# A decoder layer on one core: softmax pipeline, sample steps, output projection and weight split arranged differently

## What is computed

```
def swa_attend(q, k, v, q_pos, k_pos, sinks):        # 16 heads of 64, 4 heads share a key/value head
    s = einsum('bnqkgd,bnskd->bnkgqs', q, k) * 64 ** -0.5
    s = s - slopes * (q_pos - k_pos)                  # ALiBi; masked outside a window of 128
    m = maximum(max(s), sink)
    p = exp(s - m)
    denom = sum(p) + exp(sink - m)
    return einsum('bnkgqs,bnskd->bnqkgd', p / denom, v)

o = swa_attend(...)      # prompt: 4 blocks of 128 queries against 256 keys
                         # sample: 8 queries of each sequence against 128 cached and 8 new keys
y = x + o @ w_out
```

## Time and profile before

| what | us |
|---|---|
| median of 3 runs (1464.42 to 2238.26) | 1465.75 |
| span of the profiled execution | 1458.1 |
| TensorE matmul busy in it | 1385.9 (95%) |
| VectorE busy | 521.3 (36%) |
| ScalarE busy | 394.0 (27%) |
| GpSimd busy | 572.6 (39%) |

### The profile page before, as it was taken

The page is one execution under the profiler, slowest core; times in us unless marked ns, Lnnn a source line. Parts: engine busy times, 40 slices in busy tenths (PEclk is TensorE's granted clock), DMA queues, the critical chain, the costliest instruction groups (busy, mean ns, idle before and its releaser), DMA issues.

```text
span 1458.1 us, 23961 instructions
## 1 busy us (share of the span) xinstructions
PE 1385.9 (95%) x9812; PEld 1292.0 (89%) x9812; DVE 521.3 (36%) x886; ACT 394.0 (27%) x668; POOL 572.6 (39%) x249
## 2 busy tenths in 40 slices
PE   6888789999999999999999999979999999999995
PEld 6766538999999999999789789769999999999995
DVE  6466654621111111222125666647311111111114
ACT  3233331222222222222102534422222222222221
POOL 3422203633333333444556343327333333334441
PEclk9999858999999999999999999999999999999998
DMA  6500000222222222222322132212222222222221
GB/s 226 203 30 30 30 0 32 85 82 77 86 86 79 79 86 86 89 86 88 116 73 83 62 109 105 102 48 87 87 79 79 86 72 86 86 87 87 87 72 65
DMA packets 34341, 121.00 MB, mean 83 GB/s; under 512 B 4993, under 2 KB 6337, under 8 KB 32849
## 3 DMA queue, kind: packets, MB, share of 16 engines
q1 hardware_dynamic: 30496, 103.43, 21.7%
q10 hardware_dynamic: 3792, 16.82, 3.1%
HBM read 112.77 MB, written 9.44 MB: 84 GB/s over the span
## 4 chain that ended last, share of the span: by engine, by line
PE 70%; issue 13%; POOL 8%; DVE 7%; ACT 2%; DMA 0%; POOLq 0%; ACTq 0%; DVEq 0%
PE ps L372 22%; PE ps L374 22%; PE ps L373 22%; POOL wlo L341 4%; POOL whi L338 4%; DVE SC L844 2%; DVE SC L823 1%; ACT SC L1190 1%; PE ps L510 1%; DVE SC L820 1%; PE ps L508 1%; DVE rbc L771 1%; PE ps L501 1%; PE ps L482 0%; DVE nm L827 0%
## 5 line engine op out<-in xcount | busy, mean ns | idle before, releaser
L341 POOL TENSOR_TENSOR wlo<-wst,whi 128x1024 fp32r<-128x1024 f32 x188 | 465.1, 2474 | 505.7 <-ACT whi L1254 501.3
L372 PE MATMUL ps<-xhi,whi 128*128 128x288 f32 x1840 | 551.5, 300 | 1.9 <-DVE QT L789 0.9
L373 PE MATMUL ps<-xlo,whi 128*128 128x288 f32 x1840 | 544.7, 296 | 0.0
L374 PE MATMUL ps<-xhi,wlo 128*128 128x288 f32 x1840 | 542.8, 295 | 0.0
L372 PEld LDWEIGHTS ps<-xhi,whi 128*128 128x128 f32 x1840 | 346.7, 188 | 10.7 <-issue 9.4
L374 PEld LDWEIGHTS ps<-xhi,wlo 128*128 128x128 f32 x1840 | 348.0, 189 | 0.0
L373 PEld LDWEIGHTS ps<-xlo,whi 128*128 128x128 f32 x1840 | 347.4, 189 | 0.2
L372 PE MATMUL ps<-hhi,whi 128*128 128x288 f32 x960 | 286.0, 298 | 7.1 <-POOL wlo L341 3.3
L373 PE MATMUL ps<-hlo,whi 128*128 128x288 f32 x960 | 284.3, 296 | 0.0
L374 PE MATMUL ps<-hhi,wlo 128*128 128x288 f32 x960 | 283.4, 295 | 0.0
L338 POOL TENSOR_TENSOR whi<-wst,epsz 128x1024 fp32r<-128x1024 f32 x56 | 107.2, 1914 | 353.6 <-PE ps L374 347.4
(11 more groups left out here) (165 smaller groups left out, 1076.6 us busy)
## 6 DMA issues: line engine op xcount, KB each, us to landing
wst<-w_blocks_in SPq DMA_DIRECT2D x189, 512.0 KB, 3.3
S<-s_in ACTq DMA_DIRECT2D x4, 1024.0 KB, 4.9
s_sample_out<-S ACTq DMA_DIRECT2D x4, 1024.0 KB, 3.9
y_out<-x SPq DMA_DIRECT2D x8, 288.0 KB, 2.3
bias<-bias_in ACTq DMA_DIRECT2D x1, 2048.0 KB, 10.9
x<-x_in SPq DMA_DIRECT2D x6, 288.0 KB, 7.2
ktx<-ktx_in ACTq DMA_DIRECT2D x1, 1024.0 KB, 6.2
Vc<-vc_in ACTq DMA_DIRECT2D x1, 1024.0 KB, 13.2
```

Of the source, the lines that this page charges most:

```text
L341: nc.gpsimd.tensor_tensor(wlo[:, slot % RING, :], wst[:, slot, :], raw(whi[:, slot % RING, :]), ALU.subtract).then_inc(w_split, 1)
L372: mm(out, stat[0], mov[0], start=start, stop=False)
L373: mm(out, stat[0], mov[1], start=False, stop=False)
L374: return mm(out, stat[1], mov[0], start=False, stop=stop)
```

## The change

- A step's heads are scored one at a time into one bank (4 or 5); the second waits on the first (`first_head`). Other matmuls (`fill`) stand between. Scores of step k+1 are issued in round k, together with transposes and values of step k-1.
- Three score buffers; VectorE does `biased(k)`, then `probs(k-1)`. Scores, bias and sinks are negated (ScalarE turns the tables once), so the minimum is the exponent's bias and L827 goes. Outputs of prompt tiles alternate between banks 2 and 7.
- Sample steps hold four sequences and one key/value head each; their values come out transposed already, so the copy `OS` and `turn_out` go. Four of them stand in tile 4 between its prompt steps, four at the end.
- The first half of the output projection (4 of 8 input chunks) is cut in 16 units of 12 matmuls, issued from tile 7 on and added to x by VectorE each; the second half follows as 8 tiles of 24 matmuls.
- Weight blocks 4 to 15 are split by ScalarE (high) and VectorE (low) (`early`); GpSimd does the others as before. Small tables are loaded by SP ahead of block 4.

```
+def attention_steps():
...
+    out = [("p", n, i) for n in range(4) for i in range(NQB)]
+    for i in range(NQB):
+        out += [("p", 4, i), ("s", i)]
+    return out + [("p", n, i) for n in range(5, 8) for i in range(NQB)] + [("s", q) for q in range(4, 8)]
...
+def attention_fills():
...
+            room = [(k - 1, n > 0, 2), (k, 0, 1), (k, 1, 1), (k + 1, 0, 1), (k + 1, 1, 2), (k + 2, 0, 1)]
...
+    k = AT_STEP["p", 7, 0]
+    room = [(k - 1, 1, 1)] + [(k + i, part, 1) for i in range(4) for part in range(2)]
+    room += [(k + 4 + i, part, 2) for i in range(4) for part in range(2)]
+    room += [(NSTEP, 0, 1), (NSTEP, 1, 1), (NSTEP + 1, 0, 2), (NSTEP + 2, 0, 3)]
...
+SPLIT_AT = {6 + n: AT_STEP["p", n, 0] for n in range(6)}
+SPLIT_AT.update({12: AT_STEP["p", 6, 0], 13: AT_STEP["p", 7, 0], 14: NSTEP - 4, 15: NSTEP - 1})
...
+            def scores(k, hd):
+                bank = 4 + k % 2
...
+                    if hd == 1:
+                        pe.wait_ge(first_head, 4 * n + i + 1)
+                    ins = mm(ps[:, bank, 256 * hd + c0:256 * hd + 256], QT[q, n, i * P:(i + 1) * P],
+                             KT[q, n // GRP, k0:(i + 1) * P], start=True, stop=True)
...
+            for k in range(-1, NSTEP + 3):
+                if k + 1 < NSTEP:
+                    scores(k + 1, 0)
+                fill(k, 0)
+                if 1 <= k <= NSTEP:
+                    turn(k - 1)
+                if k + 1 < NSTEP:
+                    scores(k + 1, 1)
+                fill(k, 1)
+                if 1 <= k <= NSTEP:
+                    values(k - 1)
...
+            def early(n):
...
+                dve.wait_ge(early_hi, n + 1 - EARLY)
+                tt(wlo[:, n % RING, :], wst[:, n % STAGE, :], raw(whi[:, n % RING, :]),
+                   ALU.subtract).then_inc(early_split, 1)
...
-                    chain.link(ins)
-                    ts(nm[:, par, :], mx[:, par, :], -1.0, None, ALU.mult).then_inc(sm_done, 1)
...
+            for k in range(END):
...
+                        tt(xu, ps[:, u % 3, 0:H], xu, ALU.add).then_inc(unit_read, 1)
...
+                if k < NSTEP:
+                    biased(k)
...
+                        read_tile(("Q", n), B_Q + n, 0, cols(QT, n), -HD ** -0.5)
...
+                if 1 <= k <= NSTEP:
+                    probs(k - 1)
...
+                    if SPLIT_AT[n] + 1 == k:
+                        early(n)
```

More of the change, by code:

```diff
@@ L356, in _ @@
                 laps = (n1 - m0) // STAGE
-                with pool.Fori(0, laps) as r:
-                    for j in range(STAGE):
-                        n = m0 + j
-                        split(r * STAGE + n, n % STAGE, r + (n // STAGE + 1), False, own, r * STAGE + (k0 + n - n0))
+                if laps:
+                    with pool.Fori(0, laps) as r:
+                        for j in range(STAGE):
+                            n = m0 + j
+                            split(r * STAGE + n, n % STAGE, r + (n // STAGE + 1), False, own, r * STAGE + (k0 + n - n0))
                 for n in range(m0 + laps * STAGE, n1):
@@ L472, in scores @@
[L472 to L483 removed]
+                    q = slice(HD * hd, HD * hd + HD)
@@ new lines, in turn @@
+            def turn(k):
+                SC = SCs[k % 3]
+                pe.wait_ge(pr_done, k + 1)
+                if k >= 1:
+                    pe.wait_ge(pt_read, k)
+                if STEPS[k][0] == "p":
+                    for hd in range(2):
+                        for kc in range(0 if STEPS[k][2] else 1, 2):
+                            ins = mm(ps[:, 6, (2 * hd + kc) * P:(2 * hd + kc + 1) * P],
+                                     SC[:, hd, kc * P:(kc + 1) * P], ident[:, :], start=True, stop=True,
@@ L543, in _ @@
-            pe.wait_ge(o_lo, 16)
-            for m in range(KC):
+                    t, e = divmod(STEPS[k][1], 2)
+                    gg, bh = divmod(t, 2)
+                    h = slice((2 * gg + e) * HD, (2 * gg + e + 1) * HD)
+                    rows = slice(HD * e, HD * e + HD)
+                    if e == 0 and t >= 1:
+                        pe.wait_ge(*((o_lo, 8) if t == 3 else (os_lo, t)))
+                    mm(ps[rows, SAMPLE_BANK[t], 0:P], V[0:NS_TOK, NQB, h], PTs[0:NS_TOK, par, 1, :],
+                       start=True, stop=False)
@@ L1176, in _ @@
             act.dma_start(io["v_kept"], io["v_cache"][:, NT:WIN, :]).then_inc(s_out, 16)
+            for n in range(B_Q, B_Q + 2):
+                early(n)
+            act.wait_ge(s_attc, 16 * N_ATTC)
+            act.wait_ge(s_rows, 16 * N_ROWS)
+            fn(bias[:, :, :], bias[:, :, :], ACT.Copy, scale=-1.0)
+            fn(sbias[:, :, :], sbias[:, :, :], ACT.Copy, scale=-1.0).then_inc(bias_turned, 1)
             act.wait_ge(tile_read.sem, tile_read["K", 1])
```

477 lines of the change are left out of this document (268 added, 209 removed).

## The result

The changed kernel takes 1471.84 us (median of 20 executions, 1463.15 to 1479.37); the kernel before, on the same chip, 1463.15 (20 executions, 1458.76 to 1465.98 and one of 2238.26). The ratio is 1.0061, 95% interval 1.0043 to 1.0078: 0.6% slower, clear of the noise though small, where 1% faster was forecast. It lies 22 us above the forecast and 5 above the range. The executions of the changed kernel differ with the mean granted clock: those of 1463 us have 0.978, those of 1471 have 0.971 to 0.973, those of 1477 to 1479 have 0.966 to 0.969. The profiled one is among the shortest: 1464.09 us, span 1462.3, against a span of 1458.1 before.

The account below looks back on a forecast made before the run. TensorE was taken to lose 3.7 us a tile to VectorE, waiting for ScalarE and GpSimd. Gains of 35.2 us, less 9.3 and 7.2, less 3.5 for the clock, gave 15.2: 1450 us, range 1436 to 1467.

Parts of the forecast that it names:

- Part 3: Weight blocks 4 to 15 split on ScalarE and VectorE: hidden under TensorE's work, except a 2.0 us wait for block 15.
- Part 5: Second projection half and first FFN tile: VectorE bounds, accumulation ending behind GpSimd's work, 3.2 to 5.5 us per addition, 32.4 us.
- the allowance for the clock: Attention stretch: with less idling, 7 of some 20 us at the lower clock level remain, counted as 3.5 us.
- Part 1: Prompt steps: with the deeper pipeline VectorE no longer waits for exponentials; 1.65 us of TensorE idling per tile stays.
- Part 2: Prompt steps' scores: one head alone costs what two cost together, 0.63 us, adding 2.3 us per tile, 18.5 for eight.
- Rival (a): Prompt steps' scores: a head alone costs half, so Part 2 is 6.4 us, not 18.5; 1438 us, chance 0.20.
- no scaling over 1 us: Sign of being right in the new profile: none of VectorE's scalings in the attention takes over 1 us.
- Part 4: Sample steps: four in tile 4 add 9.3 us there; tile 7 to first FFN tile takes 78.9 instead of 114.1.
- Rival (b): Clock stays low from sample step 4 on, 29.5 us more: 1480 us, slower by 1%, chance 0.08.
- Rival (c): Splits and reads fall on VectorE's chain in each tile, uncovered: ten blocks, 23 us, 1473 us, chance 0.09.
- The sum: Whole kernel: gain of 15.2 us on a span of 1458.1 gives 1443, plus 7.6 from span to median: 1450 us.

Follow-up runs that it names:

- the version with all three edits: Changed kernel with heads scored side by side, blocks 16 to 19 split by ScalarE and VectorE, and query tile 5 spread over tile 4's steps: 1438.57 us, ratio 0.9846.

## Why the prediction was wrong

Three terms were too small: a wait that was put at nothing (Part 3), the bound of the second half (Part 5), and the time at the lower clock. No one of them makes up the 22 us. Held against the forecast, stage by stage in the execution of 1464.09 us (before the allowance for the clock); a stage begins with the first work of its first round on TensorE, for tile 7 the scores of its second block (191.67), for sample steps 4 to 7 the first matmul of round 36 (210.13):

| stage | forecast | measured | off |
|---|---|---|---|
| start of tile 7 | at 189.5 | at 191.67 | +2.2 |
| tile 7 | 16.4 | 18.5 | +2.1 |
| sample steps 4 to 7 | 22.0 | 27.2 | +5.2 |
| rest of the first half, last addition | 8.1 | 11.6 | +3.5 |
| second half and first FFN tile | 32.4 | 39.5 | +7.1 |

**Part 1 was right.** VectorE no longer waits for the exponentials, and idle time is left once a tile: 1.54 us (1.03 and 0.51), for 1.65. Tiles without a fall take 17.4 to 17.7 us, for 18.15. What wasn't seen is what this idle time does: it is what the clock falls on. And VectorE's waits for ScalarE, which the deeper pipeline was for, were the smaller part of the loss in the kernel before: with the split alone its tiles were 14.4 to 15.2 us apart.

**Part 2 was right**, and it was the largest cost that an edit brought back: 0.63 us for one head, as the earlier trace rows had it; undone, 1.9 to 2.1 a tile and 13 us or more in sum. Rival (a) is refuted by the same rows.

**Part 3 failed in its mechanism.** "GpSimd idles in the attention, so the earlier trace rows don't recur" holds up to 228 us and not beyond. The ring releases block 16 to GpSimd when block 14 has been used, and that is within the last sample step; a scaling took 1.87 us, where "no scaling over 1 us" was the sign of being right. The step had 2.0 us for block 15, and with GpSimd held back it is 2.09; the wait was 5.72. The other 3.6 us, and the lower clock behind them (13.7 us for 3.4), are the +5.2 and the larger part of the +3.5 of the table: 7.3 of these 8.7 us are gone in the profile with GpSimd held back. Of the execution's time 4.2 came back, since block 16 was then split beside the second half. Splits of blocks 4 to 14 on ScalarE and VectorE cost nothing that was found, and in the kernel before those of 4 to 11 bring 10 us.

**Part 4 was right in its work and wrong in its clock.** Tile 4 with four sample steps took 32.8 us for 27.4, since 17.1 us of it were at the lower clock. That is 5.4 too many, and the tiles around it gave 3 of them back, so 2.2 stand in the first row of the table. Tile 7 has the wait for `hlo` (1.15 us), which the forecast had not, and a fall of 3.4 us behind it (201.5). Sample steps 4 to 6 took 5.0 to 5.12 us for 5.1.

**Part 5 was right in its mechanism and too small.** VectorE behind GpSimd is the bound. But the forecast let only the accumulation be held up, and `xlo` is as well: 6.38 and 6.48 us for an output tile where 5.5 was the upper end. With the projection's blocks on ScalarE and VectorE only 0.6 us of the 7.1 came back (2.6 against the run that holds block 16 back), since GpSimd then split the FFN's first two blocks beside the same output tiles. So which share of the 7.1 is GpSimd's is not measured; that `xlo` and `acc` beside it take 1.2 and 2.2 us longer is.

**The clock.** 7 us at the lower level were allowed for, 41 are there in a short execution and 75 in a long one (65 in the profile of the kernel before). Part of it is in the stages above already. Rival (b) named the right engine state and the wrong place: in the short execution sample steps 4 to 6 were at full clock. The long executions reach 1477 to 1479, near its 1480, through falls in tiles 1 to 4 and in tile 7; that is not the way it forecast, so that the number is near is luck. Rival (c) was wrong: with TensorE's work in each step the chain isn't late.

**The sum** was made against one execution and put 7.6 us on top, the distance of a median of three. An execution lies some 1.8 us above its own span (1464.09 and 1462.3), and by twenty executions the median of the kernel before is 1463.15 and not 1465.75, 5.0 above the span. The changed kernel has a spread of its own, 8 us from the profiled execution to the median. For the span, 1443 was forecast and 1462.3 measured: 16.6 in the stages up to 288.44 (20.1 off, less the 3.5 allowed for the clock), and 2.7 behind them. There the profile has three falls of 3.4 us (710.1, 805.7 and 972.9), where that of the kernel before has one of 6.8 (706.7); that explains less than 2 of the 2.7.

**Not tried apart:** the deeper pipeline, the new layout of the sample steps and the split of the projection were never run alone, so what each of them brings or costs is known only through the rows.

## What to carry to other kernels

Before a helper engine is counted as idle, look up what releases its next piece of work, and what stands in the other engine's queue at that moment; here a split that nobody needed for 20 us held up one that TensorE was waiting for. When work is moved out of a stage, ask what it covered there: half of the projection's matmuls were the cover of VectorE's additions. And of five changes made together, run each alone: two thirds of one of them were worth 10 us alone, the one with the heads cost more than that, and with the two losses undone and the fills spread the version is 1.5% faster than the kernel before, 1438.57 us, and 1.9% with the useless matmuls, 1433.81.

## What the runs showed of the hardware

A TensorE that is idle once in 16 to 18 us for 1.5 to 2.0 us (1.03 and 0.51 above, 1.67 to 2.01 in the version with all three edits), and busy for 94% of the time, can have its granted clock fall behind each such idle time (0.97 or 0.85 in the same 58 us of the same kernel). It isn't the same in each execution: 1463 and 1479 us for the same program. Ten matmuls of 1.30 us on data of no use, in that place, made the best version 4.8 us faster by its median (6 executions each, with ranges that overlap), and the changed kernel 5.0 (1471.84 to 1466.87), of which only the longer executions are the reason (shortest 1463.15 and 1462.64). What decides whether a fall ends after 3.4 us or holds for 20 to 37 stays open.

GpSimd holds VectorE up in four forms that take all their operands from SBUF: a scaling of 136 columns 1.87 us for 0.29, a product of 64 columns 2.38 for 0.23, `xlo` 2.03 for 0.82, `acc` 2.91 for 0.75. In these rows the VectorE operation lasts as long as the rest of GpSimd's operation, and at most its own time more. The addition with one operand from PSUM keeps its 0.75 to 0.76 us beside GpSimd.

One head's scores (64 rows, two matmuls of 256 columns) take TensorE 0.62 us, and two heads' side by side, in two banks, 0.63.
